# Where a loop's branch and table loads stand on TensorE, and the order of an expert's loads, in a routed mixture of experts

## What is computed

```python
def moe_ffn(h, w_router, b_router, w_gate, b_gate, w_up, b_up, w_down, b_down):
    logits = h @ w_router + b_router
    top_val, top_exp = lax.top_k(logits, TOP_K)          # 4 of 32 experts for each token
    gate_w = softmax(top_val)
    # the tokens of an expert are gathered, and for each of them
    gt = minimum(xb @ w_gate[e] + b_gate[e], 7.0)
    up = clip(xb @ w_up[e] + b_up[e], -7.0, 7.0)
    y = (gt * sigmoid(1.702 * gt) * (up + 1.0)) @ w_down[e] + b_down[e]
    # weighted by gate_w and summed for each token; then residual and layer norm
```

## Time and profile before

| | us |
|---|---|
| median of 3 runs | 1771.18 (1770.12 to 1771.64) |
| the profiled execution, its own time | 1774.28 |
| its span, first to last instruction | 1772.4 |
| TensorE busy | 1506.0 |
| VectorE busy | 628.7 |
| mean granted TensorE clock | 0.922 of full speed |

### The profile page before, as it was taken

How to read it: one execution, slowest core, us unless ns; L and a number is a source line. 1 busy time by engine, 2 the same in 40 slices (tenths; PEclk the granted TensorE clock), 3 DMA queues, 4 the chain that set the end, 5 groups by cost and what they waited for, 6 DMA issues and landing times. The chain is left out here.

```text
span 1772.4 us, 39756 instructions
## 1 busy us (share of the span) xinstructions
PE 1506.0 (85%) x14019; PEld 591.9 (33%) x14020; DVE 628.7 (35%) x2331; ACT 242.6 (14%) x671; POOL 307.0 (17%) x228
## 2 busy tenths in 40 slices
PE   6999989889559956878879998997999998979881
PEld 3444445545313311222223332332333332323220
DVE  1147865556823211212213232231323322222225
ACT  1012255630100000000000000000000000000000
POOL 0010001115312110111112211121221211212113
PEclk8999889999679988989989998998999998989896
DMA  9721246741556999999997699869699687495992
GB/s 347 176 74 45 107 165 244 220 171 48 216 199 247 400 407 408 402 403 405 371 404 283 237 345 394 300 242 397 258 332 343 230 297 304 167 406 172 402 367 96
DMA packets 178905, 488.93 MB, mean 276 GB/s; under 512 B 40376, under 2 KB 59892, under 8 KB 177845
## 3 DMA queue, kind: packets, MB, share of 16 engines
q1 hardware_dynamic: 162164, 469.54, 68.9%
q0 software_dynamic: 16704, 18.92, 5.3%
HBM read 474.60 MB, written 17.96 MB: 278 GB/s over the span
## 5 line engine op out<-in xcount | busy, mean ns | idle before, releaser
L1073 PE MATMUL banks<-arena,master 128*32 128x512 f32 x5248 | 672.4, 625 | 149.6 <-DMA arena<-in_w_up 66.3
L1095 PE MATMUL banks<-arena,master 128*32 128x256 f32 x5248 | 343.5, 392 | 2.5 <-DVE master L1767 2.5
L1787 DVE TENSOR_SCALAR master<-banks 128x256 f32<-128x256 f32 x82 | 34.8, 424 | 821.0 <-PE banks L1073 821.0
L1073 PEld LDWEIGHTS banks<-arena,master 128*32 128x32 f32 x5248 | 143.0, 111 | 465.3 <-issue 263.1
L663 POOL DMA_INDIRECT master<-moe_input,misc x84 | 93.9, 1118 | 915.1 <-DVE misc L1755 894.3
L1095 PEld LDWEIGHTS banks<-arena,master 128*32 128x32 f32 x5248 | 157.2, 112 | 143.8 <-issue 63.0
L679 POOL DMA_INDIRECT moe_output<-master,misc x82 | 130.3, 1589 | 102.4 <-issue 97.7
L835 PE MATMUL banks<-arena 128*128 128x512 f32 x256 | 112.6, 595 | 0.0
L1327 ACT ACTIVATE master<-banks 128x256 f32<-128x256 f32 x82 | 31.5, 384 | 590.2 <-PE banks L1082 590.2
L1735 DVE TENSOR_SCALAR master<-cbias 128x128 bf16<-128x128 f32 x340 | 95.1, 343 | 44.7 <-issue 44.1
L1322 ACT ACTIVATE master<-master 128x256 f32<-128x256 f32 x82 | 34.1, 416 | 533.9 <-DVE master L1787 533.9
(11 more groups left out here) (309 smaller groups left out, 1274.0 us busy)
## 6 DMA issues: line engine op xcount, KB each, us to landing
arena<-in_w_gate SPq DMA_DIRECT2D x256, 512.0 KB, 12.2
arena<-in_w_up SPq DMA_DIRECT2D x256, 512.0 KB, 15.1
arena<-in_w_down SPq DMA_DIRECT2D x128, 1024.0 KB, 13.8
arena<-in_w_ada SPq DMA_DIRECT2D x12, 2048.0 KB, 13.1
arena<-in_x SPq DMA_DIRECT2D x2, 2048.0 KB, 8.5
arena<-in_w_in SPq DMA_DIRECT2D x2, 2048.0 KB, 10.0
master<-bias_by_distance SPq DMA_DIRECT2D x16, 256.0 KB, 5.0
arena<-in_w_in SPq DMA_DIRECT2D x8, 256.0 KB, 4.4
```

The costliest lines, as they stand in the source:

```text
L1073: last = nc.tensor.matmul(two(bank[0][strip(j), :]), hTe[:, k % 2, strip(k // 2)], arena[:, 24 * b + 2 * k:24 * b + 2 * k + 2, quarter(j)] ...
L1095: last = nc.tensor.matmul(bank[1][strip(j), 0:256], actT[:, c, strip(q)], DN(b, q, c)[:, quarter(j)], start=(q == 0 and c == 0), stop=(q = ...
```

## The change

The same products are computed on the same data in the same order. On TensorE the loop is cut at another place: an iteration now begins between an odd item's gate/up products k = 6, 7 and the transposes of the next rows, and covers items 2i and 2i+1. Its four table loads stand together at its head, and none stands within it. Two table values (number of items, number of pairs) are now loaded behind item 1, and the part behind the last item is written out.

On SyncE an expert's bias row is sent in front of its first slot, both wait for group k = 1 of the last user, and the first down load has moved behind the wait for the second down group and behind the down bias. VectorE writes the table entries accordingly.

```diff
@@ SyncE, the loop over experts
-                done7 = sp.value_load(done7_i[0:1, ds(x, 1)], min_val=7, max_val=7 * NX)
+                done7 = sp.value_load(done7_i[0:1, ds(x, 1)], min_val=8, max_val=7 * NX + 1)
                 b = sp.value_load(base_i[0:1, ds(x, 1)], min_val=0, max_val=1)
                 first = b * 24
-                sp.wait_ge(s_wg[0], x * 32)
+                sp.wait_ge(s_bg, x * 16)
                 sp.wait_ge(s_gu, done7)
-                gate_up_load(0, e, first, 0)
-                sp.wait_ge(s_bg, x * 16)
-                gate_up_load(0, e, first, 1)
-                sp.wait_ge(s_gu, done7 + 1)
                 bias_load(s_bg, 0, 512, e, ds(b, 1))
-                for k in range(1, KC):
+                for k in range(KC):
                     if k == KC - 1:
                         sp.wait_ge(s_a, done)
                     elif k > 1:
-                        sp.wait_ge(s_gu, done7 + k)
+                        sp.wait_ge(s_gu, done7 + (k - 1))
                     sp.wait_ge(s_wg[k], x * 32)
                     for m in range(2):
                         gate_up_load(k, e, first, m)
-                sp.wait_ge(s_dn, done * 3)
-                sp.wait_ge(s_wd[0], x * 16)
-                down_load(0, e, first)
                 sp.wait_ge(s_dn, done * 3 + 1)
                 sp.wait_ge(s_bd, x * 16)
                 bias_load(s_bd, 512, 768, e, ds(b, 1))
-                for q in range(1, 4):
+                for q in range(4):
@@ TensorE
+            def land(m):
+                return pe.value_load(land_i[0:1, ds(m, 1)], min_val=0, max_val=NE - 1)
+
+            def next_rows(m):
+                pe.wait_ge(s_g, m * 16 + 32)
+                rows_transposed()
+                pe.wait_ge(s_oh, m + 3)
+                pe.wait_ge(s_idx, m + 2)
+                slots()
+
+            def gate_up_begins(b, m, at):
+                pe.wait_ge(s_urd, m)
+                pe.wait_ge(s_bg, at * 16 + 16)
+                pe.wait_ge(s_xe, m + 1)
+                gate_up(b, 0, at * 32 + 32)
+                gate_up_bias(b)
+                for k in (1, 2, 3):
+                    gate_up(b, k, at * 32 + 32)
+                activations_transposed(m + 1)
+                for k in (4, 5):
+                    gate_up(b, k, at * 32 + 32)
+
+            def item_body(b, m, at, at1, at2):
+                next_rows(m - 1)
+                for q in (2, 3):
+                    down(b, q, at2 * 16 + 16)
+                gate_up_begins(b, m, at)
+                down_begins(1 - b, at1 * 16 + 16, m, m + 1)
+                for k in (6, 7):
+                    gate_up(b, k, at * 32 + 32)
+            next_rows(0)
+            gate_up_begins(1, 1, 1)
+            down_begins(0, 16, 1, 2)
+            for k in (6, 7):
+                gate_up(1, k, 64)
+            n_items = pe.value_load(ends_i[0:1, 0:1], min_val=NE, max_val=NX)
+            n_pairs = pe.value_load(ends_i[0:1, 1:2], min_val=NE // 2, max_val=NX // 2)
+            with pe.Fori(1, n_pairs) as i:
+                at2, at1, at, after = (land(i * 2 + n) for n in (-2, -1, 0, 1))
+                item_body(0, i * 2, at, at1, at2)
+                item_body(1, i * 2 + 1, after, at, at1)
...
-                land = pe.value_load(land_i[0:1, ds(m, 1)], min_val=0, max_val=NE - 1)
-                back = pe.value_load(land_i[0:1, ds(m - 1, 1)], min_val=0, max_val=NE - 1) * 16 + 16
...
-            with pe.Fori(0, n_whole) as i:
-                item_body(i * 2 + 1, 1)
-                item_body(i * 2 + 2, 0)
-            item_body(n_last, 1)
```

More of the change, by code:

```diff
@@ L1154, in item_body @@
                 slots()
-                for q in (2, 3):
-                    down(1 - b, q, back)
-            with pe.Fori(0, n_whole) as i:
-                item_body(i * 2 + 1, 1)
-                item_body(i * 2 + 2, 0)
-            item_body(n_last, 1)
+            def gate_up_begins(b, m, at):
[11 more added lines that the diff above has]
+                next_rows(m - 1)
+                for q in (2, 3):
+                    down(b, q, at2 * 16 + 16)
[14 more added lines that the diff above has]
+                item_body(1, i * 2 + 1, after, at, at1)
+            pe.wait_ge(s_g, n_items * 16 + 16)
+            rows_transposed()
+            pe.wait_ge(s_oh, n_items + 2)
+            pe.wait_ge(s_idx, n_items + 1)
+            slots()
+            for q in (2, 3):
+                down(0, q, 16 * NE)
             activations_transposed(n_items + 1)
@@ L1713, in _ @@
             nc.vector.scalar_tensor_tensor(WP[:, 0:NX], parity, second, Wf, ALU.is_equal, ALU.mult).then_inc(s_selb, 1)
-            nc.vector.tensor_scalar(ends_i[0:1, 1:2], pairs[0:1, :], -1.0, None, ALU.add)
-            nc.vector.tensor_scalar(ends_i[0:1, 2:3], pairs[0:1, :], 2.0, -1.0, ALU.mult, ALU.add)
+            nc.vector.tensor_copy(ends_i[0:1, 1:2], pairs[0:1, :])
             nc.vector.tensor_scalar(ends_i[0:1, 0:1], pairs[0:1, :], 2.0, None, ALU.mult)
@@ L1725, in _ @@
             nc.vector.tensor_copy(done_i[0:1, :], bank[6][0:1, 384:416])
-            nc.vector.tensor_scalar(done7_i[0:1, :], bank[6][0:1, 384:416], 7.0, None, ALU.mult)
+            nc.vector.tensor_scalar(done7_i[0:1, :], bank[6][0:1, 384:416], 7.0, 1.0, ALU.mult, ALU.add)
             nc.vector.tensor_copy(base_i[0:1, :], bank[6][0:1, 416:448])
```

## The result

The changed kernel takes 1785.7 us (median of 4 runs, 1782.96 to 1789.65) where the kernel before takes 1771.4. The ratio is 1.008 with a 95% interval of 1.006 to 1.010: **14.3 us slower**, for 1785 forecast. The profiled execution's span is 1787.8 us.

The account below looks back on a forecast made before the run. It saw a relay between TensorE running alone and weight streams that bound the loop in turn. Later streams +13.3 and TensorE's part +0.4 made +13.7, say 14, on the median 1771.2: 1785 us, range 1771 to 1798.

Parts of the forecast that it names:

- (a): Boundary from even to odd item: it loses its branch and loads, nothing stays uncovered, gain 1.01 us each time.
- (b): Boundary from odd to even item: branch and four loads, 3.6 us against 2.25 of lead; 1.35 us uncovered, loss 0.95.
- covered after all: Rival at the loop's head: the sequencer's lead or overlapping loads leave nothing open; 1755 us, faster; chance 0.09.
- a queue twice as deep: Rival at the loop's head: a lead longer by 0.89 us leaves 0.46 of the 1.35 open; 1768 us; chance 0.05.
- (c): Around the pairs: loss of 2.2 us where item 21 ends, +0.2 at the front, gain of 0.8 at item 81.
- more stays open: Rival: sequencer's lead not regained or clock lowered, each pair some 0.65 us dearer; 1797 us; chance 0.13.
- (d): Expert weights: first weights at 3.25 us instead of 1.35, each stream 1.9 us later; seven on the path, +13.3.
- The streams swallow it: Rival to (d): a stream's end is set by something other than its start, so (d) is 0; 1772 us; chance 0.09.
- (e): Early bias row: its waits only turn into longer weight waits; gain 0, bound about 1 us at each of 6.
- (f): First down load, some 1.2 us later behind the second down group: the queue is no emptier, so nothing.
- item 81: Last item, now behind the loop's exit and two loads: estimated gain 0.8 us.

Follow-up runs that it names:

- the run with a fifth load: The kernel with only TensorE's loop changed, plus a fifth, unused table load behind the four at the loop's head: 1804.5 us, ratio 1.0187 to the kernel before.
- the loop alone: Only TensorE's loop changed against the kernel before, SyncE's order of loads as before: 1778.1 us, ratio 1.0045.
- the order of loads alone: Only SyncE's order of an expert's loads changed against the kernel before, TensorE's loop as before: 1781.5 us, ratio 1.0063.
- the faster loop: The changed loop with six table loads per pair, each where its value is first used: 1751.1 us with SyncE's changed order, 1743.3 us with its old one.
- the wait alone: The kernel before with only the first slot's wait moved from product group k=0 to k=1, bias row and down loads in their old places: 1778.6 us, ratio 1.0050.

## Why the prediction was right, and where its terms were off

The sign, the size and both mechanisms were right: a stall behind the branch and four loads, and streams that start later. That the total came within 1 us is in part luck: the terms were off by more, in both directions, and some stood at nothing.

**(a), the middle of a pair.** Right: 1.07 us gained each time (12.23 us from an even to an odd item's start, where it was 13.30), for 1.01.

**(b), the loop's head.** Right and close: 1.24 us of idle time for 1.35 forecast, and no overlap of the loads (the run with a fifth load). From an odd to an even item it is 13.53 us, where it was 12.69: +0.84 for +0.95. So a pair gains 0.23 us, not 0.06, 19 pairs 4.4 us. The rival "covered after all" needed less than 0.65 us open and is out; "a queue twice as deep" needed 0.46 and is out as well.

**(c), the ends of streams.** Here a term was mis-sized. The prediction saw that the lead is short behind a wait for the last slot and counted item 21 alone, at 2.6 us; it measures 2.50. But TensorE now waits for the last slot in items 25, 37 and 65 too, where the kernel before waited last for an earlier one, and each of those ends has the long stall (2.53, 2.53 and 2.50 us). They come with the loop alone as well (2.50 each), so it is not SyncE's order that brings them; why the last slot is now waited for was not taken apart. And the price of each is more than the stall: the down products behind all four ran at half clock for the whole or a part of their time, 3.08 to 3.64 us for 1.93. By these rows the four ends cost 1.3 + 1.2 to 1.7 us more each than an ordinary turn of the loop, 10 to 12 us, where the prediction had 1.3 more for one. The rival "more stays open" had half clock in it, but put a dearer stall at every pair; behind the front it sits at the ends of streams and under the first long one.

At the front the prediction was near with the stall before item 2 (2.46 us for 2.4), and too high with item 1's gain: its start is 1.57 us behind the transposes where it was 1.98, so 0.4 for 0.8.

**(d), the later streams.** Right in kind: first weights 3.34 us behind the item's start for 3.25 forecast, +2.0 for +1.9. Seven times that is 14, and the order of loads alone measures 11.7, in the faster loop 7.9. So not all of the shift reaches the end. The traces show where it goes. The changed kernel and the loop alone differ only in SyncE's order; laid beside each other item by item (by the start of each item's bias product), they move apart by 0.6 us from item 3 to item 22 and then, at the six later streams, by 2.2, 1.1, 1.9, 1.1, 1.2 and 2.0, and by nothing between the streams. The two kernels with six spread loads, which differ in the same way, give 0.6 and then 0.7, 1.6, 2.1, 1.0, 1.0 and 2.4. So the first, long stream swallows most of its shift, a later one on average a quarter of it, and the term of 13.3 is about 10 in both pairs. That the wait for k=1 has the greater share and the bias row's issue the smaller is likely by their lengths (1.33 of the 2.0 us), and not shown by the times. "The streams swallow it" is out.

**(e), the early bias row.** The waits for it went (41.6 to 0) and the weight waits grew by 24 us. No run has the early row by itself; the order of loads with it (1781.5 us) is no faster than the wait alone without it (1778.6), which agrees with no gain.

**(f), the down loads.** Right: nothing that can be told from 0.

The sum, term by term. The loop's terms are from the loop alone against the kernel before, (d) from the changed kernel against the loop alone, all by item starts in one profiled execution of each:

| | forecast | in the traces |
|---|---|---|
| (d) seven streams start later | +13.3 | +10.1 |
| 19 pairs on the path | −1.2 | −4.4 |
| (c) end of item 21 | +2.2 | +3.5 |
| (c) ends of items 25, 37, 65, beyond an ordinary turn | 0 | 0.0 + 2.2 + 3.5 |
| front, items 0 to 3 | +0.2 | +1.9 |
| under the first long stream, items 3 to 21 | 0 | +1.4 |
| streams that open at items 43, 69, 75, loop alone | 0 | −2.1 |
| item 81 | −0.8 | −0.2 |
| together | +13.7 | +15.9 |

The spans of the two profiled executions differ by 15.4 us, the medians by 14.3, and that of the kernel before is itself 3 us above its median, so a term can be off by a microsecond or more. But the pattern is plain: the forecast had some 8 us too many in the streams and the pairs, and some 11 too few at the ends of streams, at the front and under the first stream. The errors nearly cancel. It is the ends and the front that keep the loop alone from the gain of its pairs. At the end of item 25 the long stall costs nothing beyond an ordinary turn, although its rows show it; the kernel before had half clock of its own there (its 16 down products at 926.02 took 1.95 us, where they take 1.05 in the loop alone).

The Trainium skill's queue of 64 instructions (TensorE: Matmul & The Clock Gate, "Architectural detail: the array is 16× 32×32, not 1× 128×128") does not give the lead of this kernel: the case with so long a lead would have left 0.46 us open and 1.24 are. The Trainium skill's floor of 600 ns for a `tensor_load` (DMA: Bandwidth & Descriptors, "Latency and other measured facts") is not seen either: 298 to 307 ns, and a fifth load adds 0.67 us to a stall with all its arithmetic.

## What to carry to other kernels

Ask not only what stands behind a cover but how much stands behind one: four loads of 0.75 us, each hidden where its value is first used, cost nothing here, and the same four in a row with the branch cost a stall of 1.24 us even behind the longest cover that the loop has. Read the sequencer's own rows: the first one behind a run of products tells the lead, and the work less the lead gave the stall to about a tenth of a microsecond (3.6 less 2.25 for 1.24). And where a burst of transfers is released by a compute engine and later waited for, the wait in front of the first transfers is on the path: 2.0 us later at seven streams cost 8 to 12 us.

## What the runs showed of the hardware

TensorE's clock can fall to its lower level behind short idle stretches. In the changed kernel it never did behind a stall of 1.23 to 1.28 us (28 of 28), and behind the front it did after all ten stalls of 2.5 us; with the fifth load it did after 13 of 29 stalls of 1.9 us. Each time the next 32 down products take 2.9 to 3.6 us instead of 1.93, so such a fall costs 1.0 to 1.7 us on top of the stall in these products alone.

The length of the stall alone does not decide it. At the front 2.46 us of idle time were followed by 1.93 us of products, as were 2.02 us in the loop alone (before 707.71) and 2.53 us with the fifth load (before 1117.61). With the fifth load the stalls of 1.9 us from item 48 to item 62 bring the fall in every second turn. In the kernel before, the clock had fallen behind two waits of 1.39 and 1.48 us that end 3 us apart (755.56 and 758.48; the 8 products at 758.48 take 1.93 us for 1.06). The long stalls behind the front also stand close behind waits for weights, so the runs don't separate the stall from what came before it.
